# A mixture-of-experts step on one core: five staging places behind the weight ring, filled early and copied into their slots by GpSimd

## The chip, the cores and the metric

The kernel runs on one core of a Trainium2 chip. The metric is the device time of one execution in microseconds; the lower, the better. A core has a matrix engine (TensorE, PE in the profile), a vector engine (VectorE, DVE), an activation engine (ScalarE, ACT), a general engine (GpSimd, POOL) and a sync engine (SyncE, SP) whose queue mostly issues DMAs. Each engine runs its own instructions in order and meets the others only at semaphores.

## The reference, cut to what matters

One layer is computed for 256 prompt tokens and 32 sample tokens, all in float32, model width 1024:

```python
h  = RMSNorm(x) * (1 + scale1(c)) + shift1(c)
m  = sigmoid(h Wg_a) * pool_mix(h w_in) + sigmoid(h Wg_b) * conv_mix(h w_in)
x  = x + gate1(c) * (m @ w_out)
h2 = RMSNorm(x) * (1 + scale2(c)) + shift2(c)
# mixture of experts, 4 of 32 for each token
for e in range(32):
    gt  = min(h2 @ exp_w_gate[e] + bg, 7);  up = clip(h2 @ exp_w_up[e] + bu, -7, 7)
    act = gt * sigmoid(1.702 * gt) * (up + 1)
    out = out + combine[:, e] * (act @ exp_w_down[e] + bd)
x  = x + gate2(c) * out
y  = RMSNorm(x) * final_g
```

Each expert has three 1024 x 1024 float32 matrices, 12 MB together, so the 32 experts bring 384 MB that must be read from memory once. The rest of the weights is 44 MB.

## The kernel before, in words

**Front.** Everything up to `h2` and the router is called the front here. Its weights (45 pieces of up to 1 MB) stream through `ring`, twelve slots of 1 MB each (`RING = 12`, a slot is 128 partitions x 2048 floats). Piece `f` goes to slot `f % 12`. The last front pieces lie in slots 0 to 8.

**Items.** The router gives each expert its tokens; an item is up to 64 tokens of one expert. An expert with more than 64 tokens has two items that use the same weights. `base_i[e]` is the first item of expert e, `owner_i[n]` the expert of item n. In this run there are 33 items: one expert, the fifteenth, has two (the text writes item 14 and item 15 for them, counting from 0).

**The loop.** TensorE goes through the items in one hardware loop. An item's twelve pieces are pieces 0 to 3 of `exp_w_gate`, 4 to 7 of `exp_w_up` and 8 to 11 of `exp_w_down`; piece i of any expert always lies in slot i. `product` (the matmuls of L1306) takes one piece after another. Between the products stand other matmuls: `scatter` (L1329) adds the last item's result, `gather` (L1277 to L1289) collects the tokens of the next item, and transposes turn the activations (L1361), the tokens (L1296) and the one-hot matrices (L1373). So an item is: pieces 0 to 3, scatter, pieces 4 and 5, scatter, pieces 6 and 7, gather and transposes, pieces 8 to 11.

**Who orders the loads.** SP's queue is written out by hand and runs in order. Per expert it waits for each slot in turn until TensorE has counted it as used by the last item of the expert before (`piece_used`), and issues the 1 MB load (L375 to L378). GpSimd does no arithmetic in the loop. It waits for the landing of piece after piece (`slot_ld`) and passes it on to TensorE as one counter, `weights_ready` (L467 to L471).

**The other engines in the loop.** VectorE clips and multiplies the gate and up results (L954, L958, L961, L964), copies the turned activations (L967), adds scattered rows to `acc` (L931) and prepares the one-hot matrices of the next item (L940 to L951). ScalarE does the sigmoid and four copies out of PSUM.

**The end.** After the loop VectorE multiplies `acc` by `g2b` (the rows of gate2, L972) and adds it to `x` (L976); both lie in SBUF all the time. Then come the last scatter (L1383), the final norm with `fgb` (the rows of `final_g`) and the stores.

## Time and profile before

| | us |
|---|---|
| median of 3 timed runs | 1246.86 |
| lowest, highest | 1245.54, 1253.68 |
| the profiled execution, device time | 1254.28 |
| its span in the trace | 1252.3 |
| TensorE busy in it | 1202.8 (96%) |
| VectorE busy | 457.4 (37%) |
| ScalarE busy | 185.0 (15%) |
| GpSimd busy | 38.7 (3%) |

The profiled execution is one execution, 7.4 us above the median of the timed runs. Its span leaves out 2 us around the first and the last instruction. Matmul records are pipelined and their ends modelled, so 96% busy does not mean that TensorE is at its peak; a TensorE that waits a little for each piece still looks busy. The queue of SP is not counted as busy, its issues stand in the timeline as SPq.

### The profile page before, as it was taken

The page shows a single profiled execution, that of the slowest core. Times are in us where ns is not written, and L with a number is a line of the kernel's source. Part 1 is how long each engine was busy: PE and PEld are TensorE (multiplying, and loading weights), DVE is VectorE, ACT ScalarE, POOL GpSimd, SP SyncE. Part 2 cuts the span into 40 slices and gives each one's busy share as a digit, 9 for nine tenths or more (in the row PEclk, how much of TensorE's full clock was granted, in tenths as well). Part 3 has the DMA queues.
Part 4 walks back from the last instruction along what each step waited for, and adds up shares of the span by engine and source line. Part 5 has one row for each costly group of instructions (what it writes and reads, how often), then busy time and mean ns, then how long its engine had stood idle before and what let it go on. Part 6 is the DMA issues. An engine that isn't in the chain of part 4 may idle for free.

```text
span 1252.3 us, 16413 instructions
## 1 busy us (share of the span) xinstructions
PE 1202.8 (96%) x5662; PEld 452.8 (36%) x5662; DVE 457.4 (37%) x1006; ACT 185.0 (15%) x295; POOL 38.7 (3%) x58
## 2 busy tenths in 40 slices
PE   5999999999999999999999999999999999999995
PEld 1675665533333333333322333333333332222221
DVE  2498314563233222333332333233222333223326
ACT  1101300111111111111111111111111111111112
POOL 1053000100000000000000000000000000000000
PEclk9999999799999999999999999999999999999998
DMA  9958564579999999999999799999999999999994
GB/s 350 371 201 304 190 237 149 179 274 396 409 410 410 410 410 410 410 410 410 410 410 410 292 395 410 409 410 410 409 410 410 410 409 410 410 409 410 410 409 168
DMA packets 129418, 456.01 MB, mean 364 GB/s; under 512 B 8377, under 2 KB 23285, under 8 KB 126331
## 3 DMA queue, kind: packets, MB, share of 16 engines
q1 hardware_dynamic: 126960, 452.23, 91.9%
q10 hardware_dynamic: 2443, 3.58, 0.9%
q8 instruction: 9, 0.15, 0.0%
q14 instruction: 6, 0.05, 0.0%
HBM read 454.38 MB, written 1.40 MB: 364 GB/s over the span
## 4 chain that ended last, share of the span: by engine, by line
PE 70%; DMA 15%; DVE 6%; SPq 6%; ACT 1%; issue 1%; POOLq 0%; DVEq 0%
PE bank L1306 42%; DMA ring<-in_exp_w_gate 13%; PE bank L1329 7%; SPq L377 6%; DVE h L735 5%; PE bank L1277 3%; PE bank L1114 3%; PE bank L1191 2%; PE bank L1287 2%; PE bank L1018 1%; DMA ring<-in_w_ada 1%; PE bank L1296 1%; PE bank L1031 1%; PE bank L1085 1%; PE bank L1173 1%
## 5 line engine op out<-in xcount | busy, mean ns | idle before, releaser
L1306 PE MATMUL bank<-ring,arena 128*64 128x512 f32 x3168 | 713.1, 597 | 11.9 <-POOLq L471 10.1
L1306 PEld LDWEIGHTS bank<-ring,arena 128*64 128x64 f32 x3168 | 213.9, 136 | 460.8 <-issue 394.9
L931 DVE TENSOR_TENSOR arena<-arena,bank 128x512 f32<-128x512 f32 (+1 forms) x198 | 126.5, 680 | 93.6 <-PE bank L1329 93.2
L954 DVE TENSOR_SCALAR arena<-bank 128x512 f32<-128x512 f32 x33 | 22.8, 691 | 282.5 <-PE bank L1306 282.5
L1329 PE MATMUL bank<-arena 64*128 64x512 f32 (+1 forms) x396 | 106.8, 628 | 0.0
L940 DVE TENSOR_SCALAR arena<-slot_no,item_col 128x128 f32<-128x128 f32 x99 | 28.3, 343 | 139.5 <-PE bank L1373 137.7
L627 ACT ACTIVATE arena<-bank 128x512 f32<-128x512 f32 x33 | 19.7, 597 | 386.0 <-PE bank L1289 386.0
L1114 PE MATMUL bank<-arena,ring 128*128 128x288 f32 x256 | 64.9, 412 | 0.0
L1277 PE MATMUL bank<-h,arena 128*64 128x512 f32 x272 | 64.7, 597 | 0.0
L735 DVE SCALAR_TENSOR_TENSOR h<-h,dwc 128x318 f32<-128x318 f32 x120 | 61.9, 591 | 0.0
L1114 PEld LDWEIGHTS bank<-arena,ring 128*128 128x128 f32 x256 | 48.9, 193 | 16.9 <-issue 3.7
L1329 PEld LDWEIGHTS bank<-arena 64*128 64x128 f32 (+1 forms) x396 | 24.5, 158 | 78.6 <-issue 78.6
L625 ACT ACTIVATE arena<-arena 128x512 f32<-128x512 f32 x33 | 20.8, 629 | 203.5 <-DVE arena L954 203.5
L961 DVE TENSOR_SCALAR arena<-bank 128x512 f32<-128x512 f32 x33 | 22.8, 691 | 75.9 <-PE bank L1306 75.9
L1085 PE MATMUL bank<-arena,ring 128*128 128x288 f32 x192 | 47.0, 407 | 0.0
L967 DVE COPY arena<-bank 128x512 f32<-128x512 f32 x33 | 22.8, 691 | 63.0 <-PE bank L1361 63.0
L625 ACT ACT_TABLE_LOAD x33 | 42.3, 1283 | 1.0 <-issue 0.4
L1085 PEld LDWEIGHTS bank<-arena,ring 128*128 128x128 f32 x192 | 36.4, 190 | 10.4 <-issue 0.5
L1288 PE MATMUL bank<-biases,mine 32*64 32x512 f32 x136 | 37.0, 613 | 0.0
L1289 PE MATMUL bank<-h,arena 32*64 32x512 f32 x136 | 37.0, 613 | 0.0
L1287 PE MATMUL bank<-biases,mine 32*64 32x512 f32 x136 | 37.0, 613 | 0.0
L1031 PE MATMUL bank<-ring,cT 128*32 128x512 f32 x192 | 28.1, 701 | 7.5 <-DMA ring<-in_w_ada 7.5
(226 smaller groups left out, 641.9 us busy)
## 6 DMA issues: line engine op xcount, KB each, us to landing
ring<-in_exp_w_gate SPq DMA_DIRECT2D x128, 1024.0 KB, 17.9
ring<-in_exp_w_up SPq DMA_DIRECT2D x128, 1024.0 KB, 18.2
ring<-in_exp_w_down SPq DMA_DIRECT2D x128, 1024.0 KB, 18.1
ring<-in_w_ada SPq DMA_DIRECT2D x24, 1024.0 KB, 10.8
ring<-in_gate_w SPq DMA_DIRECT2D x8, 1024.0 KB, 5.5
ring<-in_w_in SPq DMA_DIRECT2D x6, 1024.0 KB, 13.2
ring<-in_w_out SPq DMA_DIRECT2D x4, 1024.0 KB, 6.4
ring<-in_conv_w_out SPq DMA_DIRECT2D x2, 1024.0 KB, 7.9
```

The source lines that it names most:

```text
L377: sp.dma_start(ring[:, i, :].rearrange("p (k n) -> p k n", k=2), w[e][:, 2 * (i % 4):2 * (i % 4) + 2, :]).then_inc(slot_ld[i], 16)
L625: a.activation(gsig, gmin, ACT.Sigmoid, scale=ALPHA).then_inc(gsig_ready, 1)
L735: ins = v.scalar_tensor_tensor(out=yc[:, c, :], in0=uc_ext[:, c, k:k + CW], scalar=tap, in1=yc[:, c, :], op0=ALU.mult, op1=ALU.add)
L931: ins = v.tensor_tensor(acc[0:r, t, cs], acc[0:r, t, cs], src, ALU.add)
L1031: ins = mm(out[32 * j:32 * j + 32, :], cT[:, k, :], ring[:, f % RING, HALF * j:HALF * (j + 1)], start=(k == 0), stop=(k == KD - 1), skip_g ...
L1085: ins = mm(bank[n % 4][:, 0:TOK], w[:, k, P * (n % 2):P * (n % 2 + 1)], hT[:, k, :], start=(k == 0), stop=(k == KD - 1))
L1114: ins = mm(bank[n % 4][:, 0:TOK], w[:, k, P * (n % 2):P * (n % 2 + 1)], hT[:, k, :], start=(k == 0), stop=(k == KD - 1))
L1277: ins = mm(bank[0][64 * hh:64 * hh + 64, :], oh[:, t, :], h2[:, t, HALF * hh:HALF * (hh + 1)], start=(t == 0), stop=False, skip_group_chec ...
L1287: mm(bank[3][out, :], mine[B_GATE, :], bias_rows[B_GATE, cs], start=True, stop=False, skip_group_check=True)
L1288: mm(bank[4][out, :], mine[B_UP, :], bias_rows[B_UP, cs], start=True, stop=False, skip_group_check=True)
L1306: ins = mm(out[64 * hh:64 * hh + 64, :], lhs(k), ring[:, s, D * (k % 2) + HALF * hh:D * (k % 2) + HALF * (hh + 1)], start=(done is y_mm an ...
L1329: ins = mm(out, ohwT[64 * hh:64 * hh + 64, P * t:P * t + ROWS[t]], ysb[64 * hh:64 * hh + 64, :], start=True, stop=True, skip_group_check=True)
```

## The change

Five more places of 1 MB stand behind the ring. They are laid over memory that is free during the loop: the end of the `arena`, then `x`, then half of `biases`. For that, all of these become parts of one tensor `big`, and `ring`, `arena`, `x` and `biases` are views of it.

- Pieces 0 to 4 of every expert but the first are loaded into the five places, pieces 5 to 11 into their ring slots as before. The queue of SP still goes through an expert's pieces from 0 to 11. It waits for places 0 to 4 until GpSimd has moved the last expert's pieces out of them (`moved`), and for slots 5 to 11 until TensorE has used them.
- GpSimd copies each of the five pieces, 128 x 2048 floats, from its place to its slot once TensorE has used the slot, and then passes it on. For the second item of an expert the source is the slot itself (`source_i` is 0): the copy is made all the same, in place. It reads one more register per item.
- Ahead of the loop SP loads the first expert's pieces in the order in which slots come free, and the second expert's pieces 0 to 4 between them, each once its memory is free.
- `x` is written to memory (`x2_rows`, 1.1 MB) after `h2` is made, and read back with `g2b` (0.6 MB) after the last item's pieces have been moved; `g2b` was loaded in the front before, by ScalarE's queue.
- VectorE makes `source_i` with two small instructions after `owner_i`, and waits for `x2_in` ahead of the additions to `x`.

```diff
+STAGED = 5
...
+        AREA = 15360
+        big = sb("big", [P, RING * SLOT + AREA + TT * D + 2 * D])
+        ring = big[:, 0:RING * SLOT].rearrange("p (s n) -> p s n", n=SLOT)
...
+        STAGE = RING * SLOT + 9216
...
-            def expert(e, last_use):
-
+            def load(e, i):
...
+                w = (wg_v, wu_v, wd_v)[i // 4]
+                dst, done = ((big[:, STAGE + SLOT * i:STAGE + SLOT * (i + 1)], stage_ld[i])
+                             if i < STAGED and not (isinstance(e, int) and e == 0) else (ring[:, i, :], slot_ld[i]))
+                sp.dma_start(dst.rearrange("p (k n) -> p k n", k=2),
+                             w[e][:, 2 * (i % 4):2 * (i % 4) + 2, :]).then_inc(done, 16)
+
+            by_use = sorted(range(PIECES), key=front_use)
+            for i in by_use[0:8]:
+                sp.wait_ge(piece_used, front_use(i))
+                load(0, i)
+            sp.wait_ge(cm_mm, KD)
+            load(1, 0)
+            sp.wait_ge(rows_out[0], 64)
+            sp.wait_ge(rows_out[1], 64)
+            load(1, 1)
+            for i in by_use[8:]:
+                sp.wait_ge(piece_used, front_use(i))
+                load(0, i)
+            sp.wait_ge(x2_ready, 2 * TT)
+            load(1, 2)
+            sp.wait_ge(h2_ready, TT)
+            sp.dma_start(x2_rows[0:NP_TOK, :].rearrange("(t p) d -> p t d", p=P), x[:, 0:2, :]).then_inc(x2_out, 16)
+            sp.dma_start(x2_rows[NP_TOK:TOK, :], x[0:NS_TOK, 2, :]).then_inc(x2_out, 16)
+            sp.wait_ge(x2_out, 32)
+            load(1, 3)
+            sp.wait_ge(logit_mm, 1)
+            load(1, 4)
...
+            with sp.Fori(2, E) as e:
+
+                at_1 = sp.value_load(base_i[0:1, bass.ds(e - 1, 1)], min_val=1, max_val=MAX_ITEMS)
+                at = sp.value_load(base_i[0:1, bass.ds(e, 1)], min_val=1, max_val=MAX_ITEMS)
                 for i in range(PIECES):
...
+                    if i < STAGED:
+                        sp.wait_ge(moved, at_1 * STAGED + (i + 1))
+                    else:
+                        used(at, i)
+                    load(e, i)
+
+            at = sp.value_load(base_i[0:1, E - 1:E], min_val=1, max_val=MAX_ITEMS)
+            sp.wait_ge(moved, at * STAGED + STAGED)
+            for gg, r in ((0, P), (1, NS_TOK)):
+                sp.dma_start(g2b[0:r, gg, :], mod_rows[1][gg:gg + 1, D:2 * D].broadcast_to([r, D])).then_inc(spread_ld[2], 16)
+            sp.dma_start(x_back[:, 0:2, :], x2_rows[0:NP_TOK, :].rearrange("(t p) d -> p t d", p=P)).then_inc(x2_in, 16)
...
                 for i in range(PIECES):
-                    pool.wait_ge(slot_ld[i], (e + (USES[i] + 1)) * 16)
+                    if i < STAGED:
+                        pool.wait_ge(piece_used, n_i * PIECES + (F_END - PIECES + i + 1))
+                        pool.wait_ge(stage_ld[i], e * 16 + 1)
+                        g.tensor_copy(ring[:, i, :], big[:, SLOT * i:][:, bass.ds(src, SLOT)]).then_inc(moved, 1)
+                        pool.wait_ge(moved, n_i * STAGED + (i + 1))
+                    else:
+                        pool.wait_ge(slot_ld[i], (e + (USES[i] + 1)) * 16)
                     pool.sem_inc(weights_ready, 1)
...
-            spread(g2b, 1, 1, spread_ld[2])
...
-            v.tensor_copy(owner_i[:, :], owner[0:1, :]).then_inc(owner_ready, 1)
+            v.tensor_copy(owner_i[:, :], owner[0:1, :])
+            step(v.tensor_tensor(source[0:1, 1:], owner[0:1, 1:], owner[0:1, 0:N_TAB - 1], ALU.not_equal))
+            v.tensor_scalar(source_i[:, 1:], source[0:1, 1:], float(STAGE), None, ALU.mult).then_inc(owner_ready, 1)
...
+            dve.wait_ge(x2_in, 32)
```

How the queues change is best read from the order of instructions. On SP, the loads of one expert in the loop before, from piece 3 to piece 5; every load waits for TensorE's count of used slots (a row with `ISA [waits ...]` is the wait of the load under it):

```order
L377 ISA [waits piece_used]
L377 DMA ring<-in_exp_w_gate 128x2x1024
L375 REGISTER_ALU
L377 DMA ring<-in_exp_w_up 128x2x1024 [waits piece_used]
L375 REGISTER_ALU
L377 DMA ring<-in_exp_w_up 128x2x1024 [waits piece_used]
```

The same place now. The first load is that of piece 3, the second that of piece 4, both to a place behind the ring; the third is that of piece 5, to its slot:

```order
L390 ISA [waits moved]
L390 DMA big<-in_exp_w_gate 128x2x1024
L432 REGISTER_ALU
L390 DMA big<-in_exp_w_up 128x2x1024 [waits moved]
L420 ISA
L390 DMA big<-in_exp_w_up 128x2x1024 [waits piece_used]
```

The loads to the new places wait for GpSimd and no longer for TensorE; loads 5 to 11 wait as before, and loads 0 to 4 of the next expert stand behind load 11 of this one, as before.

On GpSimd, the loop over items before, from the item's register load on; it is all waits and counts:

```order
L468 TENSOR_LOAD owner_i
L468 ISA x2
L470 ISA
L470 ISA [waits slot_ld0,slot_ld1,slot_ld2,slot_ld3,slot_ld4,slot_ld5,slot_ld6,slot_ld7,slot_ld8]
L467 REGISTER_ALU [waits slot_ld9,slot_ld10,slot_ld11]
```

The same loop now, from the second register load to the first copy, and from the last copy to the end of the loop:

```order
L529 TENSOR_LOAD source_i
L529 ISA x2
L532 ISA
L533 ISA [waits piece_used]
L534 ISA [waits stage_ld0]
L534 COPY big<-big 128x2048
...
L534 ISA [waits stage_ld4,piece_used]
L534 COPY big<-big 128x2048
L535 REGISTER_ALU
L537 ISA [waits moved]
L537 ISA [waits slot_ld5,slot_ld6,slot_ld7,slot_ld8]
L527 REGISTER_ALU [waits slot_ld9,slot_ld10,slot_ld11]
```

Five copies now stand in GpSimd's chain, ahead of the counts that TensorE waits for, and each item's first copy stands behind the landing of piece 11 of the item before.

## Rows read from the trace of the kernel before

**Rows 1.** The page: DMA share and GB/s, 40 slices of 31.3 us.

```profile
DMA  9958564579999999999999799999999999999994
GB/s 350 371 201 304 190 237 149 179 274 396 409 410 410 410 410 410 410 410 410 410 410 410 292 395 410 409 410 410 409 410 410 410 409 410 410 409 410 410 409 168
```

**Rows 2.** The chain that ended last, TensorE's pieces: start us, us, what.

```profile
233.75 5.41 PE bank L1018 x6
...
268.68 2.04 PE bank L1329 x8
...
403.44 10.45 PE bank L1306 x48
...
432.49 10.45 PE bank L1306 x48
...
679.91 2.04 PE bank L1329 x8
...
1212.21 2.04 PE bank L1329 x8
```

**Rows 3.** The same chain where it runs through DMAs, from issue to landing.

```profile
659.59 18.29 DMA ring<-in_exp_w_gate
677.97 1.94 PE bank L1306 x8
...
1099.68 18.34 DMA ring<-in_exp_w_gate
...
1161.12 18.34 DMA ring<-in_exp_w_gate
```

**Rows 4.** Timeline of SP's queue: start us, us, issues of pieces 8 to 11.

```profile
285.11 7.00 SPq L377 DMA_DIRECT2D ring<-in_exp_w_down  x4
...
725.38 7.00 SPq L377 DMA_DIRECT2D ring<-in_exp_w_down  x4
```

**Rows 5.** Windows of 5 us: busy us of the engines, clock, DMA share, GB/s.

```profile
285.00:290.00 5.00, 5.00 (x27) 1.72 (x25) 1.90 (x9) 0.49 (x1) 0.00 (x0) 1.00 0.93 341
695.00:700.00 5.00, 5.00 (x27) 1.68 (x23) 1.27 (x6) 0.49 (x1) 0.00 (x0) 1.00 0.46 184
...
725.00:730.00 5.00, 5.00 (x25) 1.67 (x23) 1.90 (x9) 0.49 (x1) 0.00 (x0) 1.00 0.96 355
```

**Rows 6.** GpSimd's groups by form: xcount, busy us, mean ns of one.

```profile
L459 POOL MEMSET arena<- 128x3072 f32 x1 | 2.7, 2658 | 4.7 <-DVE h L833 4.7
L440 POOL TENSOR_TENSOR arena<-arena 128x315 f32<-128x315 f32 x3 | 2.5, 836 | 0.2
...
L428 POOL TENSOR_SCALAR invc<-slot_no 128x16 f32<-128x16 f32 x4 | 1.1, 274 | 0.3
...
L425 POOL TENSOR_SCALAR part_no<-part_no 32x64 f32<-32x64 f32 x2 | 0.7, 369 | 0.2
...
L420 POOL CAST slot_no<-arena 128x128 f32<-128x128 int32 x1 | 0.3, 291 | 0.1
...
L422 POOL CAST part_no<-arena 128x64 f32<-128x64 int32 x1 | 0.2, 238 | 0.1
```

**Rows 7.** Timeline of GpSimd while VectorE runs the convolution.

```profile
75.13 10.40 POOL L440 TENSOR_TENSOR arena<-arena 128x317 f32<-128x317 f32 x1 [67.80 <-ACT arena L531]
```

**Rows 8.** The convolution's line on VectorE: xcount, ns min/median/max, first and last start.

```profile
L735 DVE SCALAR_TENSOR_TENSOR h<-h,dwc x120: 531/539/1109, 56.4 to 119.6; 128x318 f32<-128x318 f32 x120
```

**Rows 9.** Timeline of one item of the loop, around the activation.

```profile
424.93 0.69 DVE L964 SCALAR_TENSOR_TENSOR arena<-arena 128x512 f32<-128x512 f32 x1
...
426.84 0.66 PE L1361 MATMUL bank<-ident,arena 128*128 128x128 f32 x4
```

**Rows 10.** Timeline of the end.

```profile
1212.33 5.16 SPq L386 DMA_DIRECT2D arena<-in_final_g  x1
...
1226.45 3.48 DVE L972 TENSOR_TENSOR arena<-arena 128x1024 f32<-128x1024 f32 x3
...
1229.86 3.48 DVE L976 TENSOR_TENSOR x<-x,arena 128x1024 f32<-128x1024 f32 x3
...
1236.50 1.29 DVE L985 TENSOR_TENSOR arena<-bank,arena 128x512 f32<-128x512 f32 x2 [3.17 <-PE bank L1383]
```

**Rows 11.** The load of `fgb` (L386), from issue to landing.

```profile
DMA to landing us min/median/max: 19.6/19.6/19.6
```

More of the change, by code:

```diff
@@ L104, in build @@
         dwc = sb("dwc", [P, CT, 32])
-        biases = sb("biases", [P, 2, D])
         rw = sb("rw", [P, KD, E])
@@ L157, in build @@
         sh2b = view(4352, 2, D)
-        g2b = view(9216, 2, D)
+        g2b = big[:, STAGE:STAGE + SLOT].rearrange("p (a d) -> p a d", d=D)
+        x_back = big[:, STAGE + SLOT:STAGE + SLOT + TT * D].rearrange("p (t d) -> p t d", d=D)
+        fgb = big[:, STAGE + SLOT + TT * D:STAGE + SLOT + TT * D + D]
         acc = view(2304, TT, D)
@@ L171, in build @@
         cmp = view(0, N_TAB, E)
-        fgb = view(11640, D)
         B_GATE, B_UP = slice(E, 2 * E), slice(2 * E, 3 * E)
-        bias_rows = biases[:, 0, :]
+        bias_rows = biases[:, 1, :]
         ybuf = h2
@@ L183, in build @@
         slot_ld = [sem(f"slot_ld{s}") for s in range(RING)]
+        stage_ld = [sem(f"stage_ld{s}") for s in range(STAGED)]
+        moved = sem("moved")
+        x2_out = sem("x2_out")
+        x2_in = sem("x2_in")
         piece_used = sem("piece_used")
@@ L370, in _ @@
                 sp.dma_start(dst, src).then_inc(slot_ld[f % RING], 16)
-            def expert(e, last_use):
-                for i in range(PIECES):
-                    sp.wait_ge(piece_used, last_use(i))
-                    w = (wg_v, wu_v, wd_v)[i // 4]
-                    sp.dma_start(ring[:, i, :].rearrange("p (k n) -> p k n", k=2),
-                                 w[e][:, 2 * (i % 4):2 * (i % 4) + 2, :]).then_inc(slot_ld[i], 16)
-            expert(0, lambda i: max(f for f in range(N_FRONT) if f % RING == i) + 1)
@@ L381, in _ @@
-            sp.wait_ge(base_ready, 1)
-            with sp.Fori(1, E) as e:
-                at = sp.value_load(base_i[0:1, bass.ds(e, 1)], min_val=1, max_val=MAX_ITEMS)
-                expert(e, lambda i: at * PIECES + (F_END - PIECES + i + 1))
+            def load(e, i):
[4 more added lines that the diff above has]
+                             w[e][:, 2 * (i % 4):2 * (i % 4) + 2, :]).then_inc(done, 16)
@@ new lines, in front_use @@
+            def front_use(i):
+                return max(f for f in range(N_FRONT) if f % RING == i) + 1
+            by_use = sorted(range(PIECES), key=front_use)
[10 more added lines that the diff above has]
+                load(0, i)
@@ new lines, in _ @@
+            at = sp.value_load(base_i[0:1, 1:2], min_val=1, max_val=MAX_ITEMS)
+            for i in range(STAGED, PIECES):
+                used(at, i)
+                load(1, i)
+            with sp.Fori(2, E) as e:
+                at_1 = sp.value_load(base_i[0:1, bass.ds(e - 1, 1)], min_val=1, max_val=MAX_ITEMS)
+                at = sp.value_load(base_i[0:1, bass.ds(e, 1)], min_val=1, max_val=MAX_ITEMS)
+                for i in range(PIECES):
+                    if i < STAGED:
+                        sp.wait_ge(moved, at_1 * STAGED + (i + 1))
+                    else:
+                        used(at, i)
+                    load(e, i)
@@ L459, in _ @@
             g.memset(acc, 0.0).then_inc(acc_zero, 1)
+            for i in range(STAGED):
+                pool.sem_inc(stage_ld[i], 1)
+                pool.sem_inc(moved, 1)
             pool.wait_ge(base_ready, 1)
```

22 lines of the change are left out of this document (15 added, 7 removed).

## The prediction, made before the changed kernel ran

> **What bounds the kernel now.** I read the page's DMA line first. In the loop, from about 280 us on, the DMA engines move 410 GB/s in nearly every slice; the exceptions are the slice of 292 with the 395 after it, and the end [rows 1]. So the loop looks bound by memory. The chain of waits says it more exactly. It has two kinds of items. In one, TensorE follows itself: 403.44 to 432.49, 29.04 us an item [rows 2]. In the other it goes through DMAs of `exp_w_gate`, two experts apart 1161.12 - 1099.68 = 61.44, so 30.72 us an item [rows 3], or 2.56 us for each of the 12 pieces. That is the pace of the DMA engines: 12 MB in 30.72 us are 409.6 GB/s.
>
> TensorE is therefore 1.68 us an item faster than the weights. It starts the loop with a full ring, lives on that lead, and at last runs out of it; the item with resident weights (item 15) gives it a new lead, and it runs out again. The cost of running out can be summed with the scatter rows. Items 0 and 14 have theirs at 268.68 and 679.91 [rows 2]: 411.2 us for 14 items, of which TensorE alone needs 14 x 29.04 = 406.6, so 4.7 us are lost. Items 14 and 32 have 679.91 and 1212.21: 532.3 us for 18 items against 522.7, so 9.6 us are lost. **All that earlier weights could ever give back in the loop is 14.3 us, 1.1%.**
>
> **Where the ring holds the DMAs back.** Only at two places do they stand still: at the loop's start, and from about 697 us, when all of item 14's weights are in and TensorE still needs the slots for item 15 (184 GB/s in 695 to 700) [rows 5]. The question is how much earlier the stream of loads gets going again with five more places.
>
> **Part 1, the five places.** After each standstill a second, smaller dip follows: 341 GB/s at 285 to 290, and 355 at 725 to 730 [rows 5]. These stand exactly where pieces 8 to 11 are issued, at 285.11 and 725.38 [rows 4]. The reason is TensorE's own rhythm. It empties slots 0 to 7 in the first two thirds of the item, then it gathers and transposes and only then touches slot 8. By then the DMAs, which got slots 0 to 7 back, have already loaded them, and wait for slot 8. So the load of piece 8 starts when TensorE lets go of slot 8, and everything behind it follows at 2.56 us a piece with no gap. In the changed kernel pieces 0 to 4 are loaded up to 12.8 us earlier, and pieces 5 to 7 wait for their slots. Piece 8 waits for the same slot at the same moment, and SP's queue is in order, so nothing of the next expert can pass it. The five places bring forward loads that were never late. The stream from piece 8 on is where it was. **I take 0 for this part**, at both restarts. The bounds are -14.3 us (the lead grows by all five places, 5 x 2.56 = 12.8 us at each restart, which covers 4.7 and 9.6) and 0: loads that start no later cannot make it slower. I take the upper end, since both restarts show the dip at piece 8.
>
> **Part 2, the copies.** Five copies of 128 x 2048 floats per item. No copy of this size is in the trace. The nearest rows are the two casts, one input and one output: 291 ns for 128 elements, 238 for 64 [rows 6], so 0.83 ns an element and 0.19 us fixed, or 1.9 us a copy. The memset agrees (2658 ns for 3072 elements, 0.87). The upper bound is tensor_scalar: 274 ns for 16, 369 for 64 [rows 6], 1.98 ns an element, 4.3 us a copy. I take 1.9, since a cast is a copy but for the type.
>
> While TensorE has a lead, the copies are hidden: a slot is free 29 us before it is needed again, and five copies take 9.5. When it has run out, they are on the path. The item then waits for piece 3 of the gate (item 14 starts it at 677.97, right after the landing at 659.59 + 18.29) [rows 3]. Now landing is followed by 1.9 us of copying and, an estimate, 0.2 us for the wait on `moved`: TensorE is **2.1 us behind where it was**. A copy is shorter than the 2.56 us between landings, so nothing piles up. This is paid twice:
> - In item 14. TensorE is 2.1 us late, so it frees slot 8 in item 15 2.1 us late, and the whole second stream of loads is 2.1 us late.
> - In the last items, on top of that stream: another 2.1 us.
>
> Together +4.2 us. The in-place copies of item 15 have their slots free in good time: nothing.
>
> **Part 3, VectorE beside the copies.** In the front a tensor_tensor of GpSimd took 10.40 us [rows 7] where its like take 0.84 [rows 6], while VectorE ran its two-input instructions back to back; and one of these took 1.109 us instead of 0.539 [rows 8]. So the two block each other for whole instructions. In the loop the instruction that matters is L964, with two inputs in SBUF: it ends at 425.62 and TensorE needs it at 426.84 [rows 9], 1.2 us of slack. A copy that has just begun costs TensorE 1.9 - 1.2 = 0.7 us. Even in all 14 and 18 items that is 9.8 and 12.6 us, of which 4.7 + 2.1 and 9.6 + 2.1 are swallowed by the waits for weights that follow anyway. The copies drift by 1.68 us an item past that point and only hit it in some; I take 0, at most +3.9 us.
>
> The Trainium skill (SBUF — State Buffer, section "SBUF: two separate sides") has a rule against this change: GpSimd's port pair is shared with VectorE as an exclusive lock, held for the whole instruction, against a VectorE instruction in a two-port mode or one with two SBUF inputs. The trace's 10.40 us agrees. The skill (GPSIMD Engine Reference, "3.1 Elementwise — side-by-side cycle accounting") also gives 1.8 cycles at 1.2 GHz as the best of a plain loop; by that a copy would take, as an estimate, 3.1 us and the sum would be some +10 us; the casts here speak for less.
>
> **Part 4, front.** SP's new waits (`cm_mm`, `rows_out`, `x2_ready`, `x2_out`, `logit_mm`) hold up only SP's loads, which nobody needs before the loop: 0. The stores and loads of `x` and the early places share the DMA engines with the a2b and sh2b rows of ScalarE's queue. If these land later, VectorE makes `h2` later; behind that stand TensorE's filler matmuls, which run until 239.16 [rows 2], 4 us after VectorE is done (GpSimd's memset waits for that same `h2`). Cover for up to 4 us; I take 0. The two small VectorE instructions and the extra register loads vanish in the 4.7 us.
>
> **Part 5, end.** `g2b` and `x` now come behind piece 11 of the last expert. `fgb`, 0.5 MB, landed at 1212.33 + 19.6 = 1231.9 [rows 10, 11], so piece 11 at 1230.6; with the stream 2.1 late 1232.7. `g2b` (0.625 MB, 1.6 us) lands at 1234.3, and the three multiplications (3.48 us [rows 10]) end at 1237.8; `x` is there by 1237.2; the additions, 3.48 us too, end at 1241.3. Before, they ended ahead of L985 at 1236.50 [rows 10]; with 4.2 us added that would start at 1240.7. So VectorE is what comes last, by +0.6 us. `fgb` lands 1.3 us behind `x`, before its use.
>
> **Sum.** 0 + 4.2 + 0 + 0 + 0.6 = **+4.8 us**: 1254.28 becomes 1259.1 for the profiled execution. That one stands 7.4 us above the median of the runs; on the median the forecast is 1246.86 + 4.8 = **1251.7 us**, 0.4% more. A measurement of this kernel can tell about 1% (12.5 us) from no change.
>
> **The rivals.**
> - *Slow copies, slower than before.* If a copy takes 4.3 us, it is longer than the 2.56 between landings. Piece 3 is then ready 4 x 4.3 - 3 x 2.56 = 9.5 us after its landing, with the 0.2 that is 9.7, twice: +19.4, so 1266. The point from which it decides is 2.56 us a copy; for it speaks the tensor_scalar slope, against it the casts.
> - *The lock, slower.* If more of VectorE's work waits for copies than L964 (also L967 with a PSUM input, which TensorE needs at once), an item pays 0.7 + 1.9 = 2.6 us; in half of the 32 items 42 us, of which the waits for weights swallow 18.5: with the 4.8 about +28, 1275. For it: 10.40 us. Against: VectorE is busy only 37% and mostly reads PSUM in the loop.
> - *It works, faster.* The second dips come from something else than slot 8, and the lead grows by five places. Then -14.3 from the loop, +2.6 or so at the end: 1235. Against it: the issue times.
> - *The change doesn't do what it says.* That is my forecast for its purpose: places filled early, nothing gained.
>
> **How the numbers follow.** Forecast (+1 to +9 us): 0.58. Slow copies (+10 to +22): 0.17. Lock (+8 to +40): 0.11. It works (-14 to -3): 0.14, about half of it beyond 1%. The range takes the forecast, most of slow copies and half of the gain: 1240 to 1268. Faster by over 1%: 0.07; within 1%: 0.69; slower by over 1%: 0.24.
>
> **What would show it.** GpSimd's copy group: 160 of 1.9 us. DMA standstill after item 14 shorter, but a larger dip (near 0 GB/s for some us) right before pieces 8 to 11 are issued, in items 0 and 15, the issue itself at the same distance from the item's start. The chain in the last items: DMA, then GpSimd's copy, then TensorE. In the end VectorE waits for the DMA of `mod_rows`. I am wrong if piece 8 after the standstill is issued clearly earlier against the item's start, if copies take over 2.56 us, or if the 29.04 us of a full-lead item grow.

## The result, and the profile after

The changed kernel takes 1257.59 us, median of 20 runs, against 1251.02 for the kernel before, 20 runs (one run of the changed kernel took 3108.7 us; its other 19 lie between 1253.63 and 1263.53). **The ratio is 1.008, with a 95% interval of 1.0061 to 1.010**, so +7.6 to +12.5 us. This ratio on record isn't the quotient of the two medians; they differ by 6.6 us, 0.5%, which lies just below the interval. The profiled execution has a span of 1260.0 us and a device time of 1261.91; before it was 1254.28, so +7.6 there.

I cut each trace into three phases at the scatter of the items' first weights on TensorE: the front (to that of item 0), the loop (from there to that of item 32), the end (the rest).

| kernel | front | loop | end | span |
|---|---|---|---|---|
| before | 268.6 | 943.5 | 40.1 | 1252.3 |
| after | 268.6 | 950.0 | 41.4 | 1260.0 |

The front has not changed. The loop has lost 6.5 us and the end 1.3.

On the page of the changed kernel, the DMA share and GB/s, 40 slices of 31.5 us:

```profile
DMA  9958585539999999999999799999999999999994
GB/s 355 371 190 307 185 331 198 197 133 367 410 409 409 410 410 410 410 409 410 410 409 409 301 372 409 409 410 410 410 410 409 410 409 409 410 410 410 410 410 185
```

Against [rows 1], the standstill in the middle is 301 and 372 now, 292 and 395 before: no more bytes in the two slices together (673 against 687). The start of the loop is worse, 133 and 367 where 274 and 396 stood.

The page's costliest groups, GpSimd's copies and VectorE's one-hot line (xcount, busy us, mean ns of one, idle before and its releaser):

```profile
L534 POOL COPY big<-big 128x2048 f32 x160 | 306.7, 1917 | 674.8 <-DMA big<-in_exp_w_gate 596.9
L1008 DVE TENSOR_SCALAR big<-slot_no,item_col 128x128 f32<-128x128 f32 x99 | 58.7, 648 | 139.4 <-PE bank L1442 137.6
```

The copy is 1.917 us, the 1.9 of the forecast. Most of GpSimd's idle time ahead of the copies, 596.9 of 674.8 us, ends with the landing of weights. L1008 is the second reading. The same instruction in the kernel before:

```profile
L940 DVE TENSOR_SCALAR arena<-slot_no,item_col 128x128 f32<-128x128 f32 x99 | 28.3, 343 | 139.5 <-PE bank L1373 137.7
```

Its mean has gone from 343 to 648 ns.

The chain that ended last (start us, us, what), in item 0, in the first starving stretch, in item 14, and in the last items and the end:

```profile
266.43 2.38 DVE big L1008 x3
...
271.01 1.89 DVE big L953
...
275.45 0.69 DVE big L999
...
276.19 1.75 PE bank L1398 x4
...
568.29 18.17 DMA big<-in_exp_w_gate
...
586.70 1.93 POOL big L534
...
588.73 1.96 PE bank L1375 x8
...
681.42 1.88 POOL big L534
...
685.33 2.04 PE bank L1398 x8
...
1193.85 18.14 DMA big<-in_exp_w_gate
...
1212.24 1.88 POOL big L534
...
1214.21 1.96 PE bank L1375 x8
...
1221.48 15.73 DMA big<-mod_rows
...
1237.34 1.28 DVE big L1040 x2
...
1244.27 1.29 DVE big L1054 x2
```

From 568 on this is the pattern that was foretold: landing, copy, matmul. In [rows 3] the matmul began 0.09 us after the landing (659.59 + 18.29 = 677.88); now the landing is at 568.29 + 18.17 = 586.46 and the matmul at 588.73, 2.27 later. Item 14's scatter is at 685.33 against 679.91 [rows 2], +5.4. The end goes through the DMA of `mod_rows` (`g2b`), and L1054, the old L985, starts at 1244.27 against 1236.50 [rows 10], +7.8.

SP's queue, the issues of pieces 8 to 11 at both restarts:

```profile
288.71 6.99 SPq L390 DMA_DIRECT2D big<-in_exp_w_down  x4
...
730.82 7.00 SPq L390 DMA_DIRECT2D big<-in_exp_w_down  x4
```

Against [rows 4] that is +3.6 and +5.4. At the second restart it is as late as item 14's scatter (+5.4), so piece 8 stands where it stood against the item. Windows of 5 us, in item 0 and at the second restart (busy us and count of PE, PEld, DVE, ACT, POOL; clock, DMA share, GB/s):

```profile
265.00:270.00 5.00, 5.00 (x24) 1.45 (x22) 3.39 (x4) 0.00 (x0) 3.29 (x2) 1.00 0.00 0
270.00:275.00 5.00, 4.32 (x20) 1.06 (x16) 4.96 (x10) 0.63 (x1) 4.22 (x3) 1.00 0.00 0
275.00:280.00 5.00, 3.81 (x10) 1.07 (x12) 4.71 (x5) 0.00 (x0) 2.52 (x2) 0.66 0.58 210
...
710.00:715.00 5.00, 5.00 (x26) 1.42 (x22) 0.84 (x3) 0.00 (x0) 3.86 (x3) 1.00 0.70 279
715.00:720.00 5.00, 5.00 (x26) 1.26 (x22) 3.42 (x6) 0.63 (x1) 2.26 (x2) 1.00 0.00 0
720.00:725.00 5.00, 5.00 (x26) 1.67 (x26) 1.58 (x3) 0.00 (x0) 4.22 (x3) 1.00 0.79 238
...
730.00:735.00 5.00, 5.00 (x25) 1.68 (x23) 1.79 (x9) 0.49 (x1) 0.00 (x0) 1.00 0.58 206
```

At the second restart the DMAs work until about 713 instead of 697, since five more pieces have a place. Then they stand at 0; from the last landing to the next it is 10.5 us in both traces (698.3 to 708.8 before, 714.4 to 724.9 now), so the standstill comes 16 us later and isn't shorter. In the window right before and around the issue of piece 8 they move 206 GB/s where it was 355 [rows 5]. What the places brought forward is taken back, within one item.

What was not foretold is item 0, the first rows of the chain and of the windows: TensorE waits for VectorE, which is busy for 13.1 of 15 us and mostly does not get on. GpSimd's timeline has the reason:

```profile
266.32 1.89 POOL L534 COPY big<-big 128x2048 f32 x1 [28.55 <-issue]
268.60 1.96 POOL L534 COPY big<-big 128x2048 f32 x1 [0.39 <-POOL big L534]
270.95 1.90 POOL L534 COPY big<-big 128x2048 f32 x1 [0.39 <-POOL big L534]
273.24 1.90 POOL L534 COPY big<-big 128x2048 f32 x1 [0.39 <-POOL big L534]
275.52 2.38 POOL L534 COPY big<-big 128x2048 f32 x1 [0.39 <-POOL big L534]
```

When the loop opens, item 1's five pieces are in their places and slots 0 to 4 of the ring come free in time, so GpSimd copies five times with 0.39 us between, from 266.3 to 277.9. In just that time VectorE makes the first one-hot tiles (L1008, L953). Behind them in its queue stands L999, which adds the scattered rows and for which TensorE's second scatter waits until 276.19.

The wait is only half of the loss. TensorE's timeline of that scatter and of the product behind it, first before, then now, and one microsecond of the window view now:

```profile
274.23 1.13 PE L1329 MATMUL bank<-arena 64*128 64x512 f32 x4
275.29 3.65 PE L1306 MATMUL bank<-ring,arena 128*64 128x512 f32 x16
...
276.19 1.75 PE L1398 MATMUL bank<-big 64*128 64x512 f32 x4 [1.86 <-DVE big L999]
277.87 4.68 PE L1375 MATMUL bank<-big 128*64 128x512 f32 x16
...
277.00:278.00 1.00, 1.00 (x6) 0.13 (x4) 1.00 (x1) 0.00 (x0) 0.90 (x1) 0.50 0.99 410
```

The scatter starts 2.0 us later than before. Then the same matmuls take 0.6 and 1.0 us longer, since after TensorE's 1.86 us of idleness its granted clock is at half (1.2 of 2.4 GHz) from 276.6 to 280.0; in the kernel before it is at full speed there. Together these are 3.6 us: 2.0 for the wait, 1.6 for the clock. Item 0 takes 32.6 us; the other items with a lead take 29.0 to 29.1, as before.

So the trace's +7.8 consists of +3.6 (item 0), +1.8 (copy ahead of item 14), +1.1 (the last items) and +1.3 (end). The +1.1 is itself a difference. In the chain of the kernel before stands the load of piece 3 of the last expert:

```profile
1191.35 18.82 DMA ring<-in_exp_w_gate
```

It landed at 1210.17. Now it lands one piece behind the 1193.85 + 18.14 = 1211.99 of the chain above, at 1214.55, so the stream is 4.4 us late; the last item's scatter is 6.5 us late, so TensorE is 2.1 us behind the stream, a copy and its wait. Piece 8 at the second restart had been issued 5.4 us late, so the stream has got 1.0 us back since. Why is not worked out.

### The profile page after: what moved, and what is told of

It is laid out like the page before. It is cut to its first block, busy times and chain, and to the rows that moved or that the text cites. A ratio compares the mean times of both kernels' runs of the same rounds, so it can differ in the third digit from the quotient of the medians.

```text
span 1260.0 us, 17459 instructions
## 1 busy us (share of the span) xinstructions
PE 1205.2 (96%) x5662; PEld 453.2 (36%) x5662; DVE 538.2 (43%) x1008; ACT 185.1 (15%) x295; POOL 345.4 (27%) x218
## 4 chain that ended last, share of the span: by engine, by line
PE 63%; DMA 17%; DVE 8%; SPq 7%; issue 2%; POOL 1%; ACT 1%; DVEq 0%; POOLq 0%
PE bank L1375 38%; DMA big<-in_exp_w_gate 15%; PE bank L1398 5%; SPq L390 5%; DVE h L801 5%; PE bank L1183 3%; PE bank L1346 3%; PE bank L1260 2%; PE bank L1356 2%; POOL big L534 1%; DMA big<-in_w_ada 1%; PE bank L1100 1%; PE bank L1154 1%; DMA big<-mod_rows 1%; PE bank L1242 1%
## 5 line engine op out<-in xcount | busy, mean ns | idle before, releaser
L1375 PE MATMUL bank<-big 128*64 128x512 f32 x3168 | 714.8, 598 | 14.1 <-POOLq L538 12.2
L534 POOL COPY big<-big 128x2048 f32 x160 | 306.7, 1917 | 674.8 <-DMA big<-in_exp_w_gate 596.9
L1375 PEld LDWEIGHTS bank<-big 128*64 128x64 f32 x3168 | 214.3, 137 | 464.9 <-issue 398.8
L999 DVE TENSOR_TENSOR big<-big,bank 128x512 f32<-128x512 f32 (+1 forms) x198 | 126.5, 680 | 88.4 <-PE bank L1398 87.9
L1008 DVE TENSOR_SCALAR big<-slot_no,item_col 128x128 f32<-128x128 f32 x99 | 58.7, 648 | 139.4 <-PE bank L1442 137.6
L1022 DVE TENSOR_SCALAR big<-bank 128x512 f32<-128x512 f32 x33 | 22.8, 691 | 218.7 <-PE bank L1375 218.7
L1398 PE MATMUL bank<-big 64*128 64x512 f32 (+1 forms) x396 | 107.5, 631 | 1.9 <-DVE big L999 1.9
L1183 PE MATMUL bank<-big 128*128 128x288 f32 x256 | 64.8, 411 | 0.0
L1346 PE MATMUL bank<-h,big 128*64 128x512 f32 x272 | 64.7, 597 | 0.0
L1029 DVE TENSOR_SCALAR big<-bank 128x512 f32<-128x512 f32 x33 | 22.8, 692 | 76.2 <-PE bank L1375 76.2
L1183 PEld LDWEIGHTS bank<-big 128*128 128x128 f32 x256 | 48.9, 193 | 16.8 <-issue 3.7
L1035 DVE COPY big<-bank 128x512 f32<-128x512 f32 x33 | 22.8, 692 | 57.4 <-PE bank L1430 57.4
L1154 PE MATMUL bank<-big 128*128 128x288 f32 x192 | 47.0, 407 | 0.0
L953 DVE TENSOR_SCALAR big<-slot_no,item_col 128x64 f32<-128x64 f32 x102 | 40.8, 456 | 1.2
L1154 PEld LDWEIGHTS bank<-big 128*128 128x128 f32 x192 | 36.4, 190 | 10.4 <-issue 0.5
```

Of the source, the lines that this page charges most:

```text
L534: g.tensor_copy(ring[:, i, :], big[:, SLOT * i:][:, bass.ds(src, SLOT)]).then_inc(moved, 1)
L999: ins = v.tensor_tensor(acc[0:r, t, cs], acc[0:r, t, cs], src, ALU.add)
L1008: ins = v.tensor_scalar(ohw[:, t, :], both, item_col[:, 0, t:t + 1], item_col[:, 1, t:t + 1], ALU.is_equal, ALU.mult)
L1154: ins = mm(bank[n % 4][:, 0:TOK], w[:, k, P * (n % 2):P * (n % 2 + 1)], hT[:, k, :], start=(k == 0), stop=(k == KD - 1))
L1183: ins = mm(bank[n % 4][:, 0:TOK], w[:, k, P * (n % 2):P * (n % 2 + 1)], hT[:, k, :], start=(k == 0), stop=(k == KD - 1))
L1346: ins = mm(bank[0][64 * hh:64 * hh + 64, :], oh[:, t, :], h2[:, t, HALF * hh:HALF * (hh + 1)], start=(t == 0), stop=False, skip_group_chec ...
```

## The experiments

The kernel before ran beside each group of them; each ratio is against its runs in that group (medians 1248.61, 1246.71 and 1246.48 us) and differs from the quotient of the medians by up to 0.002. I give the phases of the traces as in the table above, since the front alone ends between 255.8 and 271.4 us in these executions.

**e1_late_copies.** GpSimd holds its item loop back until VectorE has made item 1's first tiles.

```diff
+            pool.wait_ge(actT_ev, 2)
             with pool.Fori(1, items) as n_i:
```

> The changed kernel, but GpSimd enters its loop of items only after VectorE has copied the turned activations of item 0, so no copy runs beside VectorE's work of item 0. Theory (the lock in item 0 moves both the matmuls and the restart of the loads): the issue of pieces 8 to 11 in item 0 goes back from 288.7 to about 285.1 us, item 14's scatter from 685.3 to about 682, the span falls by 3.6 us against the changed kernel, to about +4 us against the kernel before. Rival (the 3.6 us come from the two new VectorE instructions and the later owner_ready, or from the front): nothing moves, pieces 8 to 11 stay at 288.7, the span stays at +7.7 us.

Measured: 1253.15 us, ratio 1.0041 (1.0014 to 1.0067). Front 268.6, loop 947.6, end 41.6. VectorE's timeline in this kernel, at the same place of item 0, and then beside the copies of item 1:

```profile
266.44 0.86 DVE L1009 TENSOR_SCALAR big<-slot_no,item_col 128x128 f32<-128x128 f32 x3 [1.81 <-issue]
...
287.32 2.23 DVE L1009 TENSOR_SCALAR big<-slot_no,item_col 128x128 f32<-128x128 f32 x3 [4.30 <-PE bank L1443]
```

The three instructions take 0.86 us without copies and 2.38 or 2.23 beside them. At 287 nobody waits for them: the item is 29.0 us long. Pieces 8 to 11 are issued at 285.12, as in the kernel before, and item 14's scatter is at 681.79, +1.9, the copy alone. **The lock in item 0 (a copy of GpSimd holding up instructions of VectorE), with the clock that falls behind it, is therefore the 3.6 us**, and what remains is what the forecast had in its sum: 1.9 + 2.2 in the loop (item 14, last items) and 1.4 at the end, 5.5 in all against the +4.8 of the forecast. The span, though, falls by 2.2 us against the changed kernel and not by the expected 3.6: the 1.0 us that the stream gets back there is not got back here, which is most of the difference.

**e2_short_copies.** Each copy moves 64 of 2048 columns, so the experts' results are not the reference's; all transfers and waits are as after.

```diff
-                        g.tensor_copy(ring[:, i, :], big[:, SLOT * i:][:, bass.ds(src, SLOT)]).then_inc(moved, 1)
+                        g.tensor_copy(ring[:, i, 0:64], big[:, SLOT * i:][:, bass.ds(src, 64)]).then_inc(moved, 1)
```

> The changed kernel with each of GpSimd's copies cut to 64 of the 2048 columns: most of pieces 0 to 4 never reaches their slots, so the experts' results are not the reference's. Everything else (places, waits, loads) stays. Theory (all of the loss but the end is the length of the copies: 3.6 us in item 0, 1.9 in item 14, 1.1 to 1.9 in the last items): the span is within 1 us of the kernel before plus 1.3 us for the additions at the end, so about +1 to +2 us, and no gain appears although every piece arrives as early as in the changed kernel. Rival (the places do give a lead and the copies eat it): without the copies the kernel is 5 to 14 us faster than before.

Measured: 1255.44 us, ratio 1.0038 (1.001 to 1.0066). Front 271.4, loop 943.7, end 43.3. A copy takes 253 ns in the mean. Item 14 comes 411.1 us after item 0 (before 411.2), item 32 comes 532.5 after item 14 (before 532.3), as expected. This is the sharpest statement on the places: **with copies as good as free, five places give the loop nothing** and cost the end 3.2 us, where 1.3 were expected. The 2.8 us in the front are in this one execution. They are there at TensorE's hundredth matmul already (38.4 us, 35.6 in the trace of the changed kernel), ahead of every load whose order was changed, and not explained.

**e7_no_places.** No places, no copies; only the new loads of `g2b` and `x` at the end stay.

```diff
-STAGED = 5
+STAGED = 0
```

> The changed kernel with STAGED = 0: no places, no copies, all pieces straight into the ring; what stays is the order of the first expert's loads, x written and read back, and g2b, x and fgb loaded behind the last piece. Theory (the end alone costs 2 to 3.5 us, since VectorE waits for g2b and x and TensorE is not late): every item starts within 0.3 us of the kernel before relative to item 0, and the first last_results instruction comes 2 to 3.5 us later than before. Rival (the end costs nothing, or the front order costs): the extra time shows in the start of item 0, or not at all.

Measured: 1251.18 us, ratio 1.0036 (1.001 to 1.0062). Front 265.4, loop 944.1, end 44.1, so +4.0, more than expected. Its timeline, VectorE at the end:

```profile
1230.73 3.48 DVE L1034 TENSOR_TENSOR big<-big 128x1024 f32<-128x1024 f32 x3 [6.86 <-DMA big<-mod_rows]
1234.25 3.48 DVE L1039 TENSOR_TENSOR big<-big 128x1024 f32<-128x1024 f32 x3
1237.77 1.29 DVE L1048 TENSOR_TENSOR big<-bank,big 128x512 f32<-128x512 f32 x2
```

In [rows 10] the multiplications began at 1226.45 and hid under TensorE's last item. Here they wait 6.9 us for `g2b` and come out behind it. So the new loads at the end cost 4.0 us by themselves, and only 1.3 in the changed kernel: there the copies have put TensorE itself some 2 us further behind the DMAs, and the two delays overlap.

**e8_double_copies.** Each piece is copied twice, the second time without its first 8 columns.

```diff
-                        g.tensor_copy(ring[:, i, :], big[:, SLOT * i:][:, bass.ds(src, SLOT)]).then_inc(moved, 1)
+                        g.tensor_copy(ring[:, i, :], big[:, SLOT * i:][:, bass.ds(src, SLOT)]).then_inc(twice, 1)
+                        pool.wait_ge(twice, n_i * STAGED + (i + 1))
+                        g.tensor_copy(ring[:, i, 8:], big[:, SLOT * i + 8:][:, bass.ds(src, SLOT - 8)]).then_inc(moved, 1)
```

> The changed kernel with each copy made twice (the second leaves out 8 columns), so that a piece takes 3.8 to 3.9 us, over the 2.56 us between landings. Theory (piece 3 is ready 4 x 3.9 - 3 x 2.56 = 7.9 us after its landing, paid in item 14 and at the end, and the lock in item 0 doubles to about 7 us): item 14 comes 14 to 16 us later than in the kernel before, the span is 20 to 25 us longer. Rival (copies are hidden but for one length): item 14 is at most 2 x 1.9 us later than in the changed kernel, the span +12 us.

Measured: 1274.35 us, ratio 1.0216 (1.0161 to 1.0271). Front 262.9, loop 969.3, end 40.6. The span is 20.5 us longer and item 14 comes 15.1 us late, both as expected; item 0 takes 34.7 us, 5.7 more than before, where 7 were. The two copies of a piece (means 1.91 and 1.94 us) take 3.95 us with the wait between them, and the next piece's follow 4.4 us behind them (first copies at 670.00, 674.57, 678.90 and 683.29), which is more than the 2.56 between landings, so they pile up: 3 x 4.4 + 3.95 - 3 x 2.56 = 9.5, and 15.1 - 5.7 = 9.4 was measured. This is how the forecast's rival *slow copies* would have looked.

**e3_next_first and e4_next_first_late.** If the places don't help because piece 8 stands in line, the next expert's first pieces can be issued *ahead* of the wait for slot 8. Here SP loads pieces 0 to 4 of expert e+1 into the places and then 5 to 11 of e; e4 has e1's kind of wait too.

```diff
+            with sp.Fori(1, E - 1) as e:
...
+                for i in range(STAGED):
+                    sp.wait_ge(moved, at * STAGED + (i + 1))
+                    load(e, i, 1)
+                for i in range(STAGED, PIECES):
+                    used(at, i)
...
+                    load(e, i)
...
-            with sp.Fori(2, E) as e:
```

(The 1 in `load(e, i, 1)` means the next expert.)

> The changed kernel with another order on SP: in the round of expert e it first loads pieces 0 to 4 of expert e+1 into the five places, as soon as the copies have emptied them, and then pieces 5 to 11 of expert e into their slots. Theory (the five places gave nothing because the queue stood at slot 8 and nothing of the next expert could pass): after a standstill the stream starts about 4 us into the item with five pieces already in, so the lead is 9 to 12 us larger at both restarts, TensorE never runs out (29.04 us an item to the end), and the loop wins nearly all of 14.3 us, less the 3.6 us of the lock in item 0: the span is 9 to 12 us below the kernel before. Rival (the pace of the DMA engines is all that counts and places do not matter): as the changed kernel, +5 to +8 us.

> The order of the run before it, and GpSimd enters its loop only after VectorE has prepared the one-hot matrices of item 1 (mine_ready), so that those are not blocked. Theory: 2 to 3.6 us less than the run before it, 12 to 15 us below the kernel before, about 1% faster. Rival (the lock hits other VectorE instructions instead): no better than the run before it.

Measured: 1480.62 and 1481.66 us, ratios 1.1851 and 1.187. The expectation failed by far. The chain in e3:

```profile
623.91 18.20 DMA big<-in_exp_w_down
...
644.02 1.88 POOL big L535
...
653.17 1.88 POOL big L535
...
655.71 9.09 DMA big<-in_exp_w_up
...
664.89 3.68 PE bank L1376 x8
```

Most items take 38 us. Two in-order queues hold each other: GpSimd must first pass on piece 11 of e before it comes to the copies of e+1; SP must see these five copies before it may load into the places again, and behind that stand pieces 5 to 11, which TensorE needs. In the rows piece 11 has landed at 642.11, the five copies end at 655.05, 12.9 us later, and the load that was then let go lands at 664.80, another 9.8 us. TensorE has worked off what it had by 658.7 and stands idle for 6.2 us; its next eight matmuls take 3.68 us where they take 1.94 otherwise, at half the granted clock. Bandwidth was not the limit: 458 MB in 1481.7 us are 309 GB/s.

**e5_split and e6_split_late.** The same order on SP, but GpSimd passes on 5 to 7 of an item, makes the next item's copies, then passes on 8 to 11.

```diff
+                for i in range(STAGED, 8):
+                    pool.wait_ge(slot_ld[i], (e0 + (USES[i] + 1)) * 16)
+                    pool.sem_inc(weights_ready, 1)
...
+                for i in range(STAGED):
+                    pool.wait_ge(piece_used, n_i * PIECES + (F_END - PIECES + i + 1))
+                    pool.wait_ge(stage_ld[i], e * 16 + 1)
+                    g.tensor_copy(ring[:, i, :], big[:, SLOT * i:][:, bass.ds(src, SLOT)]).then_inc(moved, 1)
+                for i in range(8, PIECES):
+                    pool.wait_ge(slot_ld[i], (e0 + (USES[i] + 1)) * 16)
...
+                for i in range(STAGED):
+                    pool.wait_ge(moved, n_i * STAGED + (i + 1))
+                    pool.sem_inc(weights_ready, 1)
```

> The order next-expert-first on SP, and GpSimd's chain cut in two: for each item it first passes on pieces 5 to 7, then copies pieces 0 to 4 of the next item, then passes on 8 to 11, and only then counts the five copied pieces. So no copy stands behind the landing of piece 11. Theory (the 230 us of the two runs before were GpSimd's queue: copies behind the landing of piece 11, and SP's loads behind those copies): the loop is at TensorE's pace, 29.04 us an item, to the end; the 14.3 us are won, the lock in item 0 costs up to 3.6, and g2b and x arrive early: span 10 to 14 us below the kernel before. Rival (loading the next expert first starves pieces 5 to 11 of this one whatever GpSimd does): items of 38 us as before.

> The same with GpSimd entering the loop only after mine_ready of item 0. Theory: the first items start as in the kernel before, 2 to 3.6 us better than the run before it, 12 to 15 us below the kernel before. Rival: no difference to the run before it, since pieces 5 to 7 of item 0 are passed on late instead.

Measured: 1255.59 us, ratio 1.0074 (1.0043 to 1.0104), and 1257.28 us, 1.0091 (1.0048 to 1.0135). Loops 954.6 and 954.0. The 38-us items are gone, so the queues were their cause. But there is no gain, where 10 to 15 us were expected. In e5 item 0 takes 39.3 us: five copies with nearly nothing between them (9.25 us) hold up VectorE, TensorE waits 7.4 us for it (for L1008 of that kernel, the addition of scattered rows), and the rest is the clock, at half for 10.2 us from 265.3 on. In e6 it takes 29.3, and the items starve from item 6 on already (30.7 us each up to item 14). The chain of e6 shows what they starve for:

```profile
422.96 17.46 DMA big<-in_exp_w_up
...
453.68 17.46 DMA big<-in_exp_w_up
```

TensorE waits for this expert's pieces of `up`, 30.72 us apart, while five pieces of the next expert, which nobody needs yet, have gone ahead of them. The order buys 5 x 2.56 = 12.8 us of transfers and then keeps them in front of needed ones.

**e9_switched.** So a last form: next-first around the two restarts (experts 1 to 4 and 15 to 19), order of need elsewhere. The numbers are fixed to this routing; as a kernel it is an experiment only.

```diff
+            next_first(1, 5)
+            in_order(6, 15)
+            to_places(15, item_of(14))
+            next_first(15, 20)
+            in_order(21, E)
...
+            pool.wait_ge(owner_ready, 1)
+            for i in range(STAGED):
                 pool.wait_ge(slot_ld[i], (USES[i] + 1) * 16)
                 pool.sem_inc(weights_ready, 1)
-            pool.wait_ge(owner_ready, 1)
```

> The two orders switched by item number, fixed for this routing: next expert first on SP (and GpSimd's chain cut in two) for experts 1 to 4 and 15 to 19, right after the two standstills, and the order of need (pieces 0 to 11 of one expert, as in the changed kernel) elsewhere. GpSimd waits for mine_ready in item 0. Theory (next-first restarts the loads early, but then holds five pieces that are not needed yet ahead of those that are, 12.8 us, which is what it had won; switching back to the order of need while TensorE still has a lead frees them): TensorE never waits for weights, 29.04 us an item in all but one or two items, the loop from the first scatter to that of item 32 takes 929 to 934 us against 943.5 in the kernel before and about 954 in the two runs with next-first throughout; timed, 8 to 13 us (0.7 to 1.0%) below the kernel before. Rival (five places behind a ring of fixed slots can give nothing, in any order): loop of 943 us or more, not faster than before.

Measured: 1249.22 us, ratio 1.0009 (0.9984 to 1.0034). Front 267.0, **loop 936.6, 6.9 us less than before**, end 42.6. That is short of the expected 929 to 934, and the timed 8 to 13 us did not come. The items take 29.0 to 29.6 us until item 28; the last four take 30.2, 30.7, 30.7, 30.7. In the whole loop 7.4 us are lost, 6.1 of them there, instead of 14.3. Its window at the first switch back to order of need, and SP's timeline in it:

```profile
390.00:405.00 15.00, 14.80 (x79) 5.13 (x79) 5.21 (x14) 1.69 (x3) 3.98 (x3) 1.00 0.85 316
...
388.88 5.85 SPq L391 DMA_DIRECT2D big<-in_exp_w_up  x3
399.72 6.92 SPq L391 DMA_DIRECT2D big<-in_exp_w_down  x4
```

Here the DMAs stand still for some 3 us. SP waits for TensorE's count of used slots ahead of pieces 5 to 7 and again ahead of piece 8, issued at 399.72 when piece 6 had landed and piece 7 was about to (400.7). It does not wait for the places: those were copied out by 394.0 and come later in its queue. Slot 8 thus holds the stream back here too, only in an item in which TensorE has a lead. The places can thus give a lead, if the order of loads lets them. But 2.5 of the 6.9 us go at the end, where VectorE waits for `g2b`:

```profile
1223.35 3.49 DVE L1093 TENSOR_TENSOR big<-big 128x1024 f32<-128x1024 f32 x3 [5.32 <-DMA big<-mod_rows]
```

By these two phases 4.4 us would be left, and the timed runs show no gain (-2.0 to +4.2 us by their interval). The trace shows what takes the rest, and it is a side effect of this experiment's own edit. GpSimd now waits for `owner_ready` *ahead* of passing on item 0's first five pieces (the last lines of the diff), so TensorE starts item 0 late:

```profile
258.28 8.77 PE L1428 MATMUL bank<-big 128*64 128x512 f32 x32 [5.03 <-POOLq L581]
```

In the changed kernel the same 32 matmuls follow without a wait and take 7.09 us. So the front holds 5.0 us of waiting and 1.7 of lower clock, 6.7 us, that have nothing to do with the order of loads. Its length, 267.0, doesn't show them, since in this execution TensorE's clock was at half for 6.8 us of the front only, against 27.3 before. As an estimate from these figures, the order without this wait would come out 4.4 us below the kernel before; no run shows it.

## Why the prediction was right, and where its sum was not

The direction, the size class and the mechanism held: +4.8 us forecast, +7.6 in the profiled execution, 0.8% by the timed ratio, inside the range. The ratio's +10.0 us is just above the +1 to +9 that the forecast gave itself, the 6.6 us between the medians is in it. That the sum came this near is in part luck: 3.6 us were left out and 1.0 us, which nothing in the forecast has, came back.

- **Part 1, the places: 0.** Right, and shown twice: by e2, where the copies cost nearly nothing (0.25 us each) and the loop stays at 943.7, and by the issues of piece 8, as late as item 14's scatter. The bound of -14.3 us was a real one: e9 recovers 6.9 of it in the loop. One of the signs that the forecast named did not show: the standstill after item 14 is as long as before, only 16 us later.
- **Part 2, the copies: 1.9 us each, 2.1 at two places.** 1.917 measured. The forecast's 4.2 is 1.9 + 2.2 in e1, which has nothing else in it, and 1.8 + 1.1 in the changed kernel. There too TensorE is 2.1 us behind the stream in the last items; the 1.0 us less is the stream's. The casts were the right row to take. The Trainium skill (GPSIMD Engine Reference, "3.1 Elementwise — side-by-side cycle accounting") with its 1.8 cycles would have given, as an estimate, 3.1 us a copy; the trace says 1.9, and the measurement decides. The same section also has 1.03 cycles an element for k ≤ 2, which at 1.2 GHz would give, as an estimate, 1.8 us; the trace agrees with that figure.
- **Part 3, VectorE beside the copies: 0, at most 3.9.** The term that was mis-sized: it measured 3.6, of which 2.0 are the wait and 1.6 the lower clock behind it, which no term of the forecast had. I looked for the lock at L964 in the middle of an item, and it sat in the one-hot lines at the start of item 0, which have one SBUF input. The row for it was in reach: [rows 2] has item 0's first scatter at 268.68, the four gate slots are free by then, and the places are filled, so the copies had to fall on the start of item 0. The Trainium skill (SBUF — State Buffer, "SBUF: two separate sides") names both kinds of VectorE instruction, the two-input one and the one in a two-port mode; by that rule the one-hot lines were candidates if they run in such a mode. That they are held up the trace shows, 0.86 us against 2.38; the mode itself no view shows.
- **That a stall in item 0 is swallowed.** This step failed, and the text had what was needed to see it. Part 1 said that the stream's restart hangs on slot 8 of items 0 and 15. So a stall ahead of slot 8 in item 0 shifts every load behind it, and the later wait for weights moves along with it instead of absorbing it. Only stalls behind that point, in items 1 to 13, can be swallowed. The runs bear on that little: in e1 the copies beside item 1 stretch VectorE's three instructions to 2.23 us, but TensorE has slack and doesn't stall (the item takes 29.0); of the 0.2 us that item 2 of e1 loses, item 14 shows nothing.
- **Part 4, front: 0.** 268.6 in both traces, one execution each, with the same granted clock (0.95 in the mean of the front). The seven experiments that keep the changed kernel's places and order of work in the front have 255.8 to 271.4 us there, so a cost of a few microseconds is not excluded.
- **Part 5, end: +0.6.** 1.3 measured, and `g2b` is what comes last, as forecast. Both sides came later than assumed by the same 2.3 us: the stream 4.4 late for 2.1, TensorE 6.5 for 4.2. That moves the forecast's landing of `g2b` from 1234.3 to 1236.6. It landed at 1237.21, since it came 2.2 us behind piece 11 (1235.03) and not 1.6; by these 0.6 VectorE stood out further. e7 gives the full price, 4.0.
- **The rivals.** *Slow copies* is refuted by 1.917 us, and e8 shows its price. *The lock* was right in kind: L1008's mean of 648 ns against 343 over 99 instructions shows it in many items, but TensorE pays for it in one and not in half of them. The suspect L967, which reads PSUM, was not held up at all (L1035 now, 0.692 us in the mean against 0.691). *It works* is refuted by e2. *The change doesn't do what it says* was the forecast, and it stands.

The timed ratio, +10.0 us, is 2.4 more than the one trace's +7.6, and the difference of the medians, 6.6, is 1.0 less; so the runs don't settle whether there is more than the trace shows.

## What to carry to other kernels

More buffer helps only if the transfer that would start earlier is the next in its queue: look up which issue ends the standstill and what that waits for, here slot 8. Then count what the buffer's upkeep puts on the path (here a copy behind each landing) and sum a stall only as swallowed if the transfer stream it delays does not hang on the same event. When loads are put in another order to get past that, an engine that handles landings in order needs the same order, and loads ahead of need cost later what they gain at first.

## What the runs showed of the hardware that I had not expected

- GpSimd's copy of 128 x 2048 floats takes 1.90 us in the median (1.89 to 2.40), and 0.253 us in the mean for 128 x 64: 0.83 ns an element. Three of VectorE's tensor_scalar with one SBUF input, 128 x 128, take 0.86 us alone and 2.2 to 2.4 beside such copies.
- A copy never held up an instruction of VectorE that reads PSUM; those that read SBUF only it mostly did. In the loop of the changed kernel, by its forms:

```profile
L1032 DVE SCALAR_TENSOR_TENSOR big<-big 128x512 f32<-128x512 f32 x33 | 28.6, 866 | 1.1
L1035 DVE COPY big<-bank 128x512 f32<-128x512 f32 x33 | 22.8, 692 | 57.4 <-PE bank L1430 57.4
```

  L1032 reads SBUF only; the 8 of its 33 instructions that start while a copy runs take 1.41 us in the mean, the others 0.69. L1035 reads PSUM (`bank`); 11 of its 33 start while a copy runs, and all take 0.69. The same holds for L999, L1022 and L1029, which read PSUM too: 39 of them start beside a copy, and in the mean they take what they take alone, to 1 ns. Of those that read SBUF only, the copy of three columns (L1015) is the exception: in e1 12 of 33 start beside a copy, and none takes over 0.16.
- TensorE's granted clock shows in the times of the same kernel. In the timed runs of the kernel before, spans near 1252.5 us mostly go with a mean clock of 0.985 and spans near 1244 with 0.995; the changed kernel has 1260.0 at 0.984 and 1252.8 at 0.992. In the traces much of it lies in the front. Before the change, and after, the clock is at half for 27.3 us of the front, which is 268.6 us long (0.95 in the mean of that window); in e6 it never falls in the front (1.00), and the front is 255.8 us long. As an estimate, 27.3 us at half the clock cost up to 13.7 where TensorE is the limit; the difference is 12.8. Some microseconds differ otherwise: e3 and e5 both have 3.4 us at half and fronts of 259.8 and 256.6. The totals of one kernel can differ by 8 us for this, as much as the whole effect, so phases within a trace say more than two totals.
- Items slowed by waiting cost clock too: e3, which waits in most items, has a mean granted clock of 0.929 against 0.985. So a wait of TensorE can cost more than its length: in item 0 of the changed kernel 2.0 us later came to 3.6.
